# Moving the reciprocals of four differential heads, and one small subtraction, on VectorE in a two-layer transformer kernel

## The reference

```python
    proj = h @ w_in
    ...
        s_f = s_f + cf[..., :, None] - cum_f[..., None, :]
        p_f = jax.nn.softmax(jnp.where(causal, s_f, -jnp.inf), axis=-1)
        o_f = jnp.einsum('bhqk,bhkd->bhqd', p_f, v_f)
    ...
        p_d = jax.nn.softmax(s_d, axis=-1)
        a_d = p_d[:, :, 0] - lam * p_d[:, :, 1]
        o_d = jnp.einsum('bhqk,bhkd->bhqd', a_d.astype(v_d.dtype), v_d)
    ...
    o_d = _rmsnorm(o_d, subln) * (1.0 - lambda_init)
    return jnp.concatenate([o_f, o_d], axis=-1) @ w_out
```

## Time and profile before

| | |
|---|---|
| median of 3 runs | 2614.03 us (2612.71 to 2614.33) |
| profiled execution: its own time | 2612.88 us |
| its span, first to last instruction | 2611.1 us |
| PE busy | 2595.8 us, 99% of the span |
| DVE busy | 1426.9 us, 55% |
| ACT busy | 1023.6 us, 39% |
| POOL busy | 236.1 us, 9% |
| mean granted TensorE clock | 0.999 of full speed |
| steps 0 to 31 of a mixer | about 406 to 588 us, and again about 1374 to 1556 us |

### The profile page before, as it was taken

How to read it: one execution, slowest core, us unless ns; L and a number is a source line. 1 busy time by engine, 2 the same in 40 slices (tenths; PEclk the granted TensorE clock), 3 DMA queues, 4 the chain that set the end, 5 groups by cost and what they waited for, 6 DMA issues and landing times.

```text
span 2611.1 us, 32978 instructions
## 1 busy us (share of the span) xinstructions
PE 2595.8 (99%) x12286; PEld 2120.2 (81%) x12286; DVE 1426.9 (55%) x1874; ACT 1023.6 (39%) x1592; POOL 236.1 (9%) x173
## 2 busy tenths in 40 slices
PE   8999999999999999999999999999999999999999
PEld 7888887878888888888887778888887888888877
DVE  5444248875444335444258765444247657845773
ACT  4222135654222224222135654222235554334663
POOL 0000014201000000000024101000001110012220
PEclk9999999999999999999999999999999999999999
DMA  4222223213222223222233113222222222322221
GB/s 160 96 97 97 96 100 104 66 44 105 97 96 96 97 81 110 97 96 97 97 103 94 65 53 101 96 96 96 97 92 78 81 82 89 109 97 93 85 74 52
DMA packets 70323, 239.13 MB, mean 92 GB/s; under 512 B 8528, under 2 KB 10832, under 8 KB 70224
## 3 DMA queue, kind: packets, MB, share of 16 engines
q1 hardware_dynamic: 69792, 236.91, 26.9%
q10 hardware_dynamic: 432, 0.87, 0.1%
HBM read 230.15 MB, written 2.10 MB: 89 GB/s over the span
## 4 chain that ended last, share of the span: by engine, by line
PE 94%; DVE 2%; issue 1%; ACT 1%; POOL 0%; DVEq 0%; POOLq 0%; DMA 0%; ACTq 0%; SPq 0%
PE bank L419 21%; PE bank L421 20%; PE bank L420 20%; PE score L420 6%; PE score L419 6%; PE score L421 6%; PE flip_bank L419 2%; PE flip_bank L420 2%; PE flip_bank L421 2%; PE score L1185 1%; PE flip_bank L1213 1%; PE score L1958 1%; PE score L2785 1%; PE bank L2820 1%; PE bank L1235 1%
## 5 line engine op out<-in xcount | busy, mean ns | idle before, releaser
L393 DVE TENSOR_TENSOR w_lo<-w_raw,w_hi 128x1024 fp32r<-128x1024 f32 x425 | 526.7, 1241 | 543.1 <-ACT w_hi L353 532.3
L419 PE MATMUL bank<-h_hi,w_hi 128*128 128x512 f32 x1840 | 733.9, 399 | 0.3 <-DVE w_lo L393 0.3
L421 PE MATMUL bank<-h_hi,w_lo 128*128 128x512 f32 x1840 | 718.1, 390 | 0.0
L420 PE MATMUL bank<-h_lo,w_hi 128*128 128x512 f32 x1840 | 717.5, 390 | 0.0
L353 ACT ACTIVATE w_hi<-w_raw 128x1024 fp32r<-128x1024 f32 x427 | 447.7, 1051 | 406.7 <-DMA w_raw<-stream 406.3
L419 PEld LDWEIGHTS bank<-h_hi,w_hi 128*128 128x128 f32 x1840 | 346.2, 188 | 73.5 <-issue 2.8
L421 PEld LDWEIGHTS bank<-h_hi,w_lo 128*128 128x128 f32 x1840 | 345.7, 188 | 72.9
L420 PEld LDWEIGHTS bank<-h_lo,w_hi 128*128 128x128 f32 x1840 | 346.4, 188 | 71.2 <-issue 2.4
L553 ACT ACTIVATE hid_hi<-tmp 128x512 f32 (+1 forms) x88 | 55.6, 632 | 408.0 <-DVE tmp L778 408.0
L772 DVE TENSOR_TENSOR tmp<-bank,rstd 128x512 f32<-128x512 f32 x132 | 91.2, 691 | 148.2 <-PE bank L421 147.9
L548 ACT ACTIVATE tmp<-tmp 128x512 f32<-128x512 f32 x88 | 55.6, 632 | 248.7 <-DVE tmp L772 248.7
(11 more groups left out here) (562 smaller groups left out, 3833.4 us busy)
## 6 DMA issues: line engine op xcount, KB each, us to landing
w_raw<-stream SPq DMA_DIRECT2D x427, 512.0 KB, 3.2
tmp<-tmp SPq DMA_DIRECT2D x64, 64.0 KB, 2.0
x_tok<-x SPq DMA_DIRECT2D x4, 512.0 KB, 7.1
wx_raw<-stream SPq DMA_DIRECT2D x4, 512.0 KB, 4.6
out<-out_tok SPq DMA_DIRECT2D x8, 256.0 KB, 2.0
tmp<-qr SPq DMA_DIRECT2D x16, 64.0 KB, 2.7
tab_in_f<-tables SPq DMA_DIRECT2D x1, 704.0 KB, 10.4
cos_sin<-rope ACTq DMA_DIRECT2D x1, 512.0 KB, 4.3
```

Source lines behind the costliest of these rows:

```text
L393: nc.vector.tensor_tensor(w_lo[:, s, :], w_raw[:, s, :], w_hi[:, s, :].bitcast(F32), ALU.subtract).then_inc(lo_ready, 1)
L419: nc.tensor.matmul(dst, whi, xhi, start=start, stop=False)
L420: nc.tensor.matmul(dst, whi, xlo, start=False, stop=False)
L421: return nc.tensor.matmul(dst, wlo, xhi, start=False, stop=stop)
```

## The change

Three tables and one condition are edited. The first differential head is inverted in steps 17 to 19 (256, 128 and 128 columns) in place of 18 to 20 (128, 128, 256); the second in steps 20 and 21 (256 each) in place of 21 alone (512); the third in 22 and 24 (128, 384) in place of 22 to 24 (128, 128, 256); the fourth in 25 and 26 (256 each) in place of 25 alone (512). So the products L977 come at the ends of steps 19, 21, 24 and 26 (before 20, 21, 24 and 25), ACT's copies L676 in steps 20, 22, 25 and 27 (before 21, 22, 25 and 26), and the first head's subtraction in step 20 (before 21). And `flip_low(0)`, which stood behind `maxima(2)` in step 2, stands in step 1 behind `weigh(1)`. The only instruction more is one reciprocal in each mixer: the same 4 x 512 columns are cut in 9 parts, where there were 8.

```diff
-        LOW_AT = {21: 0, 22: 1, 25: 2, 28: 3}
+        LOW_AT = {20: 0, 22: 1, 25: 2, 28: 3}
...
-            return {20: 0, 21: 1, 24: 2, 25: 3}.get(k)
+            return {19: 0, 21: 1, 24: 2, 26: 3}.get(k)
...
-        INVERSE_AT = {18: (0, slice(0, P)), 19: (0, slice(P, 2 * P)), 20: (0, slice(2 * P, S)), 21: (1, slice(0, S)),
-                      22: (2, slice(0, P)), 23: (2, slice(P, 2 * P)), 24: (2, slice(2 * P, S)), 25: (3, slice(0, S))}
+        INVERSE_AT = {17: (0, slice(0, 2 * P)), 18: (0, slice(2 * P, 3 * P)), 19: (0, slice(3 * P, S)),
+                      20: (1, slice(0, 2 * P)), 21: (1, slice(2 * P, S)), 22: (2, slice(0, P)), 24: (2, slice(P, S)),
+                      25: (3, slice(0, 2 * P)), 26: (3, slice(2 * P, S))}
...
                     if k < NSTEP and k != 1:
                         maxima(k)
-                    if k >= 2 and is_diff((k - 2) // TB):
+                    if k > 2 and is_diff((k - 2) // TB):
                         flip_low(k - 2)
...
                         if is_diff(h):
                             v_low(h)
+                    if k == 1:
+                        flip_low(0)
                     if k < 2:
                         rope_add("qk"[k], 1)
```

## The result

The changed kernel takes 2616.97 us, median of 22 runs (2614.96 to 2620.01), against 2612.88 us of 22 runs of the kernel before (2610.37 to 2614.42). The ratio is 1.0015, with a 95% interval of 1.0009 to 1.002: slower, with the whole interval above 1, and by less than the 0.2% that the prediction took as its bound. The profiled execution took 2615.69 us with a span of 2613.9, against 2612.88 and 2611.1.

What follows compares the result with a forecast made beforehand. PE, busy 99% of the span, was taken as the bound. Terms of +0.2 - 0.6 + 1.8 = +1.4 us a mixer, +2.8 for two, gave 2615.7 from the profiled execution, 2616.8 from the median; forecast 2616.5, range 2612.0 to 2619.0.

Steps and rivals of the forecast that it cites:

- flip_low(0), +0.2 us predicted: Steps 1 to 3: `flip(1)` starts sooner, but later exponentials delay the scores of step 3, +0.20 us in a mixer.
- Steps 17 to 25, -0.6 us: Shorter reciprocal in step 21 brings `maxima(22)` 1.8 us sooner and removes PE's waits at step 23, -0.6 us in a mixer.
- The steps that were to cost nothing: Steps 17, 19, 20, 24 and 25: moved work is covered by DVE's idle time or swapped for equal work, no cost.
- Step 26, the collision, +1.1 us: Step 26: POOL's earlier `q_lo` excludes `weigh(26)`'s operations on `probs`, which end at 559.7 instead of 558.57, +1.1 us.
- maxima(27) +1.8: Behind step 26: `maxima(27)` starts at 562.2 instead of 560.38, +1.8 us.
- k_hi +2.35: Ahead of step 28: `k_hi` of group 7 comes +1.8 + 0.55 = 2.35 us later, at 565.35 instead of 562.99.
- the two waits +1.8 us: Ahead of step 28: PE waits for `k_hi` and then `k_lo`, together 1.8 us in a mixer.
- the sign: In the profile: PE waiting for `k_hi` and `k_lo` ahead of step 28, 1.5 to 2 us in a mixer.
- The first rival, no collision,: Step 26: `weigh(26)` gets ahead of POOL, PE waits 0.7 us, +0.3 in a mixer, 2614.6 us; chance 18%.
- The second,: Step 28: `k_lo` of group 7 still in time, only the waits removed count, -0.4 in a mixer, 2612.8 us; chance 17%.
- The sum, +1.4 in a mixer.: Whole mixer: +0.2 - 0.6 + 1.8 = +1.4 us, +2.8 us for two mixers.
- The clock rival: Behind step 28: the new wait of 1.8 us lowers TensorE's clock, +3.4 us on top, 2620.2 us; chance 6%.

Runs made afterwards that it cites:

- e1: Changed kernel, with POOL's `q_lo` of group 7 held until both weigh operations of step 26 are done: 2612.74 us, ratio 1.0003.
- e3: Changed kernel, with POOL's `q_lo` of group 7 held until weigh(26) is done and ACT's copy of head 3 put behind `k_hi`: 2612.45 us, ratio 0.9998.
- e4: Changed kernel, with head 3 inverted and multiplied in step 25 alone, as before the change: 2611.71 us, ratio 0.9997.
- e7: Kernel before, with head 3 alone cut over steps 25 and 26: 2618.67 us, ratio 1.0023.
- e9: Changed kernel, with all 512 columns of head 3's reciprocal in step 26: 2622.63 us, ratio 1.0037.
- e6: Kernel before, with only heads 0 and 1 in their new places: 2610.68 us, ratio 0.9993.
- e8: e6, with POOL's `q_lo` of group 1 held until both weigh operations of step 1 are done: 2610.64 us, ratio 0.9994.
- e10: e4, with POOL's `q_lo` of group 1 held until both weigh operations of step 1 are done: 2611.50 us, ratio 0.9993.
- e2: Changed kernel, with ACT's copy of head 3 put behind `k_hi` of step 27: 2614.31 us, ratio 1.0008.
- e5: Kernel before, with the move of `flip_low(0)` alone: 2613.15 us, ratio 0.9999.
- e11: Kernel before, with POOL's `q_lo` of group 1 held until both weigh operations of step 1 are done: 2612.19 us, ratio 0.9997.
- the first four experiments: e1, e2, e3 and e4, each measured beside the kernel before, whose median there was 2612.64 us.

## Why the prediction was right, and where it was off

It gave 2616.5 us with a range of 2612.0 to 2619.0, "no change" on the slow side; 2616.97 was measured. By its steps:

**flip_low(0), +0.2 us predicted.** Right in kind, and too large. Step 2 as a whole changed by -0.04 and -0.29 us in the first execution, +0.23 and -0.04 in the second, and +0.16 and -0.07 with the part alone. But most of that is the scatter of step 0 shown above, which has nothing to do with the edit. Counted from the start of the first operation of `weigh(1)` on `probs`, the turn of v stands 4.04 us behind in the kernel before and in the changed one, as the prediction held, and `exps(2)` 3.22 us before and 3.42 us after, the 0.20 us that it took. But the scores of step 3 stand 4.62 to 4.63 us behind in the six mixers with `flip_low(0)` in its old place, and 4.70 to 4.72 in the sixteen with the new one (those with POOL held in step 1 left out). So the move costs 0.08 us a mixer: behind the exponentials there were 0.12 us of slack, which the prediction put at nothing, with 0 to 0.28 us as its bounds.

**Steps 17 to 25, -0.6 us.** Measured -0.61 to -0.71 in four mixers, -0.65 and -0.72 with heads 0 and 1 alone. `maxima(22)` was put near 530.0; it stands at 529.46, or 529.9 in the time of before (the mixer began 0.45 us sooner). The steps that were to cost nothing cost nothing.

**Step 26, the collision, +1.1 us.** Measured 1.06 (e1 against the changed kernel). POOL's `q_lo` began 0.02 us ahead of the weigh operation, which took 1.48 us. By the rule that the prediction names from the Trainium skill ("SBUF — State Buffer", "SBUF: two separate sides"), whichever of the two starts first holds the pair of ports for its whole instruction; the trace agrees, as POOL's 1.28 us were not lengthened and the weigh operation ended 0.2 us behind them. That POOL's operation and a reciprocal do not hinder each other is seen in e1 and was in no term.

**maxima(27) +1.8, k_hi +2.35, the two waits +1.8 us.** In the time of before (add 1.15 us) `maxima(27)` stands at 562.03, +1.65; `k_hi` at 565.15, +2.16; the loss is 1.70 in each mixer. The printed waits add to 1.39 us, where 1.5 to 2 us were named as the sign. The small excess of the prediction lies ahead of the 2.5 us between weigh and maxima: these measure 2.49 (558.39 to 560.88), but they began at 559.54 in the time of before, where 559.7 was taken.

**The first rival, no collision,** is what e1 is: a loss of 0.64 at step 28 where that rival said 0.7. **The second,** faster by the waits removed, is e3 and e4. At step 28 both were priced about rightly, for kernels that are not this one; their whole times (+0.1 us for e1, -0.2 and -0.9 us for e3 and e4) can't be told from before.

**The sum, +1.4 in a mixer.** Measured +0.98 and +0.68 in the first execution, +1.30 and +0.96 in the second: on average +1.0. Of the 0.4 us between, step 2 has about 0.2, and the terms of steps 17 to 25 and of the two waits 0.1 each.

**The clock, and luck.** The medians lie 4.1 and 4.5 us apart, the mixers of the two profiled executions only 1.7 and 2.3. The prediction's 2616.5 hit the median in part by luck: it moved from the profiled 2612.88 up towards 2614.03, a median of three that 22 runs put at 2612.88. On that base its own sum says 2615.7, which the profiled execution met to the hundredth, and that is luck too: 1.1 us less in the mixers, 0.5 less ahead of them, 1.6 more at 1995 to 2003.

The clock rival named a mechanism that e7 and e9 show, but it acted there in no profiled execution of the changed kernel. Behind step 28 the fall came in none of four mixers of the changed kernel, in one of two of e7 with the same waits, in two of two of e9 with longer ones. The longer stretch at 1995 us isn't the change's doing as far as 14 profiled executions tell: 3.4 us were lost there in seven (both of the changed kernel, e3, e4, e6, e8, e10), 1.7 in three (before, e2, e5) and nothing in four (e1, e7, e9, e11), behind the same wait of 1.6 to 1.7 us each time.

So about 2 us of the changed kernel's median stay open. What a median adds to the growth of the two mixers of its profiled execution is 2.4 and 2.2 us for the changed kernel, and between -0.6 and +1.4 us for the eleven others. Its mean granted clock was lower, too: not one of its 33 runs had 1.000 and 16 were at 0.998 or 0.997, while of 102 runs of the kernel before beside the experiments 18 were at 1.000 and 2 at 0.998, and of 44 runs of e3, e4, e8 and e10 two were at 1.000 and one at 0.998. Falls behind step 28 in runs that were not profiled would explain it; that is argued from e7 and e9, and no trace of the changed kernel shows one.

## What to carry to other kernels

Work moved into an engine's idle gap must be measured against the gap and against what follows the gap: here 2.5 us in 1.81 us of idle time left 0.7, of which PE saw 0.16 (e3), and the two neighbours whose start moved with it (a copy on ACT, a half on POOL) made 1.70 out of that. Where POOL and VectorE work close together, read the length of each VectorE operation in a timeline, not its mean; one that takes three times its usual time beside a POOL operation can be cured with one wait on POOL, if POOL's result isn't wanted at once. When a stretch scatters, follow the engine that is late back to where it last was idle: the cause lay two steps ahead of the wait that showed it. Try the parts of a composed change alone: here one third of it carried the whole loss and another all of the gain.

## What the runs showed of the hardware

- A TENSOR_SCALAR on 128x384 that began 0.02 us behind a POOL operation took 1.48 us in place of 0.42, and one on 128x256 that began 0.55 us behind one took 1.15; each ended 0.2 us after POOL. In step 0 operations on 128x128 took up to 1.49 us in place of 0.35. RECIPROCAL on 128x256 took 1.74 us beside POOL as alone, and the TENSOR_TENSOR that reads PSUM (`sqsum<-bank`, 128x512) 0.68 us beside POOL's `k_lo` (from 418.76 and 418.72 us in the changed kernel), as alone.
- The granted clock fell behind waits of the same printed size (0.8 and 0.6 us) in one mixer of six, and behind 2.4 and 0.6 us in two of two. One fall there cost 1.6 to 1.7 us. Behind the wait of 1.65 us near 1993 us it cost nothing, 1.7 us or 3.4 us, in four, three and seven of 14 profiled executions. A good part of the 4 us by which one kernel's runs differ can be read from their mean clock: of the kernel before, beside the first four experiments, 8 runs at 1.000 had a median of 2611.11, 24 at 0.999 one of 2612.72.
